# First block of a fused transformer kernel: input columns reordered, attention and gating worked between the chunks of the input projection, rotation read from PSUM on VectorE, retention last

## The chip, the cores and the metric

The kernel runs on one core of a Trainium2 chip. The metric is the device time of one execution in microseconds (us). TensorE is called PE, VectorE DVE, ScalarE ACT, GpSimd POOL, SyncE SP.

## The reference

A sequence of 256 tokens with 1024 channels passes through two layers of a first block (and then through a second block, which this change leaves as it is). Cut to what matters:

```python
def hybrid_layer(x, cos, sin, ...):
    h = rms_norm(x, g_mix_pre)
    z = h @ w_in                                   # 1024 -> 3200 columns
    rq, rk, rv, rg, aq, ak, av, gu, gv = split(z, [384]*7 + [256]*2)
    y_ret = silu(rg) * retention(rope(rq), rope(rk), rv)      # 6 heads of 64, group-normed
    y_att = dilated_attention(rope(aq), rope(ak), av)         # 6 heads of 64, causal softmax
    y_gm  = spatial_gating(gelu(gu), gelu(gv), w_s, b_s)      # u * (W_s norm(v) + b)
    y = concat([y_ret, y_att, y_gm])
    x = x + rms_norm(y @ w_out, g_mix_post)
    h = rms_norm(x, g_ffn_pre)
    gate, up = split(h @ w_gate_up)
    return x + rms_norm((silu(gate) * up) @ w_down, g_ffn_post)
```

A conditioning vector is also multiplied with `w_mod_2`, in three thirds for each layer ("mod0" to "mod2"), for use in the second block.

## The kernel before, in words

All arithmetic is float32. To run it on PE as three passes, each operand is cut into a high and a low part: high*high, high*low, low*high (lines 463 to 465 of `products`). Tokens are two tiles (t = 0, 1) of 128.

Weights stream in pieces called granules, two blocks of 128 rows by one chunk's columns. SP loads them in the order of a list, `ring`, into 8 raw slots (`load`, L418); a slot is loaded again only when the granule in it has been cut, or, for a mod granule (used uncut), multiplied. SP works through the list in order, so a slot that is not free holds up all later loads. ACT cuts the high part (`cut_high`, L426, or L429 with a gain), DVE the low part (`cut_low`, L436 or L439), into 4 slots: granule n can be cut only when PE is done with granule n-4.

A layer runs in this order. The input projection has 8 chunks of 400 columns in the order of `w_in`, 4 granules each; ACT copies each finished chunk from PSUM to `z`, scaled by the root of the norm (`take_z`, L2531). POOL rotates the retention columns and later the attention columns from `z` (`rope_tile`, L814 to L821). Retention is worked between chunks 3 to 7: transposes (L849), scores (L998, L999), decay on DVE (L1019), values (L925 to L927). After the last chunk `mix_pe`, `mix_act` and `mix_dve` do the rest: 24 transposes of the attention heads (L866), their cutting, then for each head scores (L1050, L1052), mask and maximum on DVE (L1207 to L1210), exponential on ACT (L1114, L1116), division on DVE (L1201), transposes (L1060), a copy by ACT (L1122), values (L1069 to L1071). The gating (gelu, norm, `wsT` product L1086) and mod0 (rows L953, columns L963) stand between the heads. Then y is transposed (L915), cut (L1129, L1234), and the output projection runs: 8 granules of 512 columns, the last four in two passes, one for each token tile, in `boundary_pe`. There mod1 rows (L953) stand between the last output and the first chunk of the feed-forward weights. Each engine's instructions run in the order written; DVE and ACT keep three granules ahead (`Cuts.to`).

PSUM has 8 banks. The chunks alternate between banks (0, 1) and (2, 3), named `MM`; the rest serve transposes, scores and outputs.

Of the kernel before, what the change touches and what calls it, by code (L numbers as in the profile page):

```python
# [7 lines left out]
F32 = mybir.dt.float32  # L8
# [163 lines left out]
def program(nc, a, out, tables):  # L172
    where = Where()
    ctx = ExitStack()
    with ctx:
# [22 lines left out]
        turned, turned_pool = xn[:, 0, 0:2 * RW], xn[:, 1, 0:2 * RW]  # L198
        logits = turned.rearrange("p (b s) -> p b s", b=2)
# [4 lines left out]
        a_q, a_k_high = hT_high, hT_low  # L204
# [19 lines left out]
        with mixer:  # L224
            z = sb("z", [P, NT, ZW], of=mixer)
            y = sb("y", [P, NT, D], of=mixer)
            qk = sb("qk", [P, NT, 4 * RW], of=mixer)
            qkT = sb("qkT", [P, NH, SEQ], of=mixer)
            a_k_low = sb("a_k_low", [P, NH, SEQ], F32R, of=mixer)
            seen = sb("seen", [P, NH, 384], of=mixer)  # L230
            gel = sb("gel", [P, NT, 2 * GMW], of=mixer)
            gel2 = sb("gel2", [P, NT, 2 * GMW], of=mixer)
            silu = sb("silu", [P, NT, RW], of=mixer)
            probT = sb("probT", [P, 2, 384], of=mixer)
        with ffn:
# [103 lines left out]
        IN_W, IN_CHUNKS, GU_CHUNKS = 400, 8, FK // 2  # L339
# [22 lines left out]
        MOD_LAST = (4, 5, 7, 8)  # L362
        OUT_ORDER = [(j, PAIRS[h]) for hs in ((0, 1), (2, 3)) for j in range(2) for h in hs]
# [4 lines left out]
        for layer in range(DEPTH):  # L368
            add_in(layer, range(1, IN_CHUNKS))
            add_mod(layer, 0)  # L370
            for j, rows in OUT_ORDER:
                w_out[layer].add(a["w_out"][layer], rows, 512 * j, 512).half = j
            add_mod(layer, 1, (0,))
# [258 lines left out]
        def x_root_pool(e, side, t, layer):  # L632
# [25 lines left out]
        def x_high_act(e, side, t, banks, layer):  # L658

            for j in range(2):  # L660
                e.wait_ge(pe.sem, pe.value(f"{side}_T{t}{j}", layer=layer))
                src, to = turned_half(t, j, banks)
                e.activation(hT_high[to], src, ACT.Copy).then_inc(act.sem, act.mark(f"{side}_H{t}{j}", layer))

        def x_low_dve(e, side, t, banks, layer):

            for j in range(2):
                e.wait_ge(act.sem, act.value(f"{side}_H{t}{j}", layer=layer))
                src, to = turned_half(t, j, banks)
                e.tensor_tensor(hT_low[to], src, hT_high[to].bitcast(F32),  # L670
                                ALU.subtract).then_inc(dve.sem, dve.mark(f"{side}_L{t}{j}", layer))
# [152 lines left out]
        def rope_tile(e, mine, t, z0, to, name, tmp, places=None):  # L824

            if t:
                e.wait_ge(mine.sem, mine.value(f"{name}{t - 1}"))
            src = heads(z[:, t, z0:z0 + 2 * RW], 2 * NH)
            dst = src if places else heads(to, 2 * NH)
            rope(e, mine, src, dst, 2 * NH, HD, cosf[:, t, :], sinf[:, t, :], tmp, f"{name}{t}", places)  # L830
# [6 lines left out]
        RT = (4, 5, 6)  # L837
        AT = (7, 6, 0, 1, 2, 3)

        def pairs_turn_pe(e, name, mine, first, banks, free):  # L840

            for t in range(NT):
                e.wait_ge(mine.sem, mine.value(f"{name}{t}"))
            for j in range(3):
                free(j)
                for pp in range(2):
                    for t in range(NT):
                        c = (first + 2 * j + pp) * P
                        last = e.transpose(PS[:, banks[j], pp * SEQ + t * P:pp * SEQ + (t + 1) * P],  # L849
                                           qk[:, t, c:c + P], ident)  # L850
                last.then_inc(pe.sem, pe.mark(f"{name}_T{j}"))

        def pairs_take_act(e, name, first, banks):
            for j in range(3):
                e.wait_ge(pe.sem, pe.value(f"{name}_T{j}"))
                c = first + 2 * j
                e.activation(qkT[:, c:c + 2, :], PS[:, banks[j], :].rearrange("p (a s) -> p a s", a=2),
                                      ACT.Copy).then_inc(act.sem, act.mark(f"{name}_qkT{j}"))

        def pairs_of_heads_pe(e):  # L860

            for i in range(NH):
                for half in range(2):
                    for t in range(NT):
                        h = 2 * i + half
                        last = e.transpose(PS[:, AT[i], half * SEQ + t * P:half * SEQ + (t + 1) * P],  # L866
                                           qk[:, t, h * P:(h + 1) * P], ident)
                last.then_inc(pe.sem, pe.mark(f"a_heads{i}"))

        def a_place(i):  # L870
            return slice(2 * (i % 3), 2 * (i % 3) + 2), PS[:, AT[i], :].rearrange("p (k s) -> p k s", k=2)

        def heads_high_act(e):
            e.wait_ge(granules_done, w_in[where.layer].last.cut + 1)
            for i in range(NH):
                e.wait_ge(pe.sem, pe.value(f"a_heads{i}"))
                ks, src = a_place(i)
                if i < 3:
                    last = e.activation(a_q[:, ks, :], src, ACT.Copy, scale=HD ** -0.5)
                else:  # L880
                    last = e.activation(a_k_high[:, ks, :], src, ACT.Copy)
                last.then_inc(act.sem, act.mark(f"a_high{i}"))

        def heads_low_dve(e):
            for i in range(NH):
                e.wait_ge(act.sem, act.value(f"a_high{i}"))
                ks, src = a_place(i)
                if i < 3:
                    rows = a_q[HD:P, ks, :]
                    last = e.scalar_tensor_tensor(rows, src[HD:P], HD ** -0.5, rows.bitcast(F32), ALU.mult, ALU.subtract)  # L890
                else:
                    last = e.tensor_tensor(a_k_low[:, ks, :], src, a_k_high[:, ks, :].bitcast(F32), ALU.subtract)
                last.then_inc(dve.sem, dve.mark(f"a_low{i}"))

        YB, OB, GB = (4, 5), (6, 7), 4

        Y_PLACES = ((0, 0), (0, SEQ), (1, 0), (OB[0], 0), (OB[0], SEQ), (OB[1], 0), (2, 0), (2, SEQ))


        Y_UNITS = (((0, 1), "y_T0"), ((2,), "y_T1"), ((3, 4), "y_T1"), ((5,), "y_T1"), ((6, 7), "y_T3"))  # L900

        def y_ready(e):
            def before(k, stream):
                if any(k == ks[0] for ks, _ in Y_UNITS):
# [2087 lines left out]
```

## Time and profile before

| | us |
|---|---|
| Three runs: lowest, median, highest | 1142.06, 1147.05, 1149.88 |
| Time of the profiled execution | 1141.9 |
| Its span, from the first to the last instruction | 1140.1 |
| PE busy (share of the span) | 1082.1 (95%) |
| DVE busy | 709.5 (62%) |
| ACT busy | 576.3 (51%) |
| POOL busy | 131.6 (12%) |

The profile is of one execution. Around its span lie 1.8 us. A busy PE is one with a product in its pipe; the ends of its instructions are modelled, so 95% says little of how fast products follow each other. That is read from their starts.

### The profile page before, as it was taken

The numbers are of one execution on the slowest core, as the hardware profiler recorded it, in microseconds if no ns is written. First come the engines' busy times: TensorE is split into PE (matmuls) and PEld (weight loads), VectorE is DVE, ScalarE is ACT, GpSimd is POOL, SyncE is SP. The second block draws the span as 40 slices with busy tenths as digits, with TensorE's granted clock in tenths as the row PEclk, the third lists the DMA queues.
The fourth block names the chain that finished last, engine by engine and source line by source line (L and its number), as shares of the span: only waits on it lengthen the run. The fifth ranks groups of instructions, "written<-read, shape, count | busy, mean of one in ns | idle before, by whom it ended". The sixth has DMA issues, their size and how long they took to land.

```text
span 1140.1 us, 15629 instructions
## 1 busy us (share of the span) xinstructions
PE 1082.1 (95%) x5974; PEld 893.2 (78%) x5974; DVE 709.5 (62%) x1162; ACT 576.3 (51%) x1054; POOL 131.6 (12%) x126
## 2 busy tenths in 40 slices
PE   7997899999999998799999999999998999999997
PEld 6896678888887997577888778889796678789785
DVE  5868756666545758766666536623256653876664
ACT  6644556555435554455555544434235643524772
POOL 1424010000001406001000000001000002022040
PEclk9999999999999999899999999999999999999999
DMA  8753568666665663459756494323211011344000
GB/s 299 238 146 95 188 202 274 185 184 182 186 182 196 227 174 109 154 177 351 234 178 184 138 343 138 86 84 116 74 57 55 1 57 56 129 124 136 1 2 37
DMA packets 109571, 170.45 MB, mean 150 GB/s; under 512 B 7213, under 2 KB 72762, under 8 KB 109242
## 3 DMA queue, kind: packets, MB, share of 16 engines
q1 hardware_dynamic: 107424, 161.92, 45.0%
q0 software_dynamic: 1440, 6.10, 1.5%
q10 hardware_dynamic: 634, 1.44, 0.3%
q8 instruction: 47, 0.77, 0.3%
q14 instruction: 26, 0.21, 0.1%
HBM read 168.39 MB, written 1.05 MB: 149 GB/s over the span
## 4 chain that ended last, share of the span: by engine, by line
PE 81%; DVE 12%; ACT 3%; issue 2%; DMA 1%; SPq 1%; DVEq 0%; POOLq 0%; POOL 0%; ACTq 0%
PE PS L463 16%; PE PS L465 16%; PE PS L464 16%; DVE low L439 5%; PE PS L2900 4%; PE PS L2901 4%; PE PS L2902 4%; PE PS L953 2%; PE PS L1699 1%; PE PS L1806 1%; PE PS L1382 1%; PE PS L1687 1%; PE PS L1644 1%; DVE low L436 1%; DMA ws_rows<-w_s 1%
## 5 line engine op out<-in xcount | busy, mean ns | idle before, releaser
L463 PE MATMUL PS<-high,hT_high 128*128 128x512 f32 (+3 forms) x860 | 329.9, 384 | 14.2 <-DVE low L439 7.8
L464 PE MATMUL PS<-low,hT_high 128*128 128x512 f32 (+3 forms) x860 | 324.2, 377 | 0.0
L465 PE MATMUL PS<-high,hT_low 128*128 128x512 f32 (+3 forms) x860 | 323.9, 377 | 0.0
L439 DVE SCALAR_TENSOR_TENSOR low<-raw,vec_cols,high 128x512 fp32r<-128x512 f32 (+1 forms) x304 | 232.9, 813 | 93.9 <-ACT high L429 93.8
L429 ACT ACTIVATE high<-raw,vec_cols 128x512 fp32r<-128x512 f32 (+1 forms) x304 | 190.1, 675 | 104.8 <-PE PS L465 102.3
L436 DVE TENSOR_TENSOR low<-raw,high 128x1024 fp32r<-128x1024 f32 (+2 forms) x118 | 139.0, 1186 | 162.9 <-ACT high L426 162.3
L426 ACT ACTIVATE high<-raw 128x1024 fp32r<-128x1024 f32 (+2 forms) x122 | 124.4, 1028 | 171.7 <-PE PS L465 92.3
L463 PEld LDWEIGHTS PS<-high,hT_high 128*128 128x128 f32 x860 | 162.0, 188 | 48.4 <-DVE low L439 14.1
L465 PEld LDWEIGHTS PS<-high,hT_low 128*128 128x128 f32 x860 | 161.9, 188 | 25.6
L464 PEld LDWEIGHTS PS<-low,hT_high 128*128 128x128 f32 x860 | 162.1, 188 | 23.6
L2900 PE MATMUL PS<-high,fT_high 128*128 128x512 f32 x176 | 70.4, 400 | 0.0
L2901 PE MATMUL PS<-low,fT_high 128*128 128x512 f32 x176 | 69.5, 395 | 0.0
L2902 PE MATMUL PS<-high,fT_low 128*128 128x512 f32 x176 | 69.5, 395 | 0.0
L463 PE MATMUL PS<-high,cT_high 128*128 128x512 f32 (+2 forms) x124 | 46.1, 372 | 0.0
L464 PE MATMUL PS<-low,cT_high 128*128 128x512 f32 (+2 forms) x124 | 45.9, 370 | 0.0
L465 PE MATMUL PS<-high,cT_low 128*128 128x512 f32 (+2 forms) x124 | 45.8, 369 | 0.0
L2900 PEld LDWEIGHTS PS<-high,fT_high 128*128 128x128 f32 x176 | 33.0, 188 | 11.0 <-issue 2.5
L621 POOL TENSOR_TENSOR norms<-norms,half_power 128x1 f32<-128x1 f32 x8 | 4.4, 552 | 318.8 <-DVE norms L613 318.8
L2902 PEld LDWEIGHTS PS<-high,fT_low 128*128 128x128 f32 x176 | 33.0, 187 | 8.1
L2901 PEld LDWEIGHTS PS<-low,fT_high 128*128 128x128 f32 x176 | 33.0, 188 | 7.6
L2253 DVE CUSTOM_DVE_ANT_0 z_late<-PS,consts,stats 128x512 f32<-128x512 f32 x32 | 22.8, 748 | 18.4 <-PE PS L1817 18.4
L2567 ACT ACTIVATE fT_high<-PS 128x512 fp32r<-128x512 f32 x22 | 13.2, 599 | 41.5 <-PE PS L2884 41.5
(359 smaller groups left out, 1560.7 us busy)
## 6 DMA issues: line engine op xcount, KB each, us to landing
raw<-w_gate_up SPq DMA_DIRECT2D x176, 256.0 KB
raw<-w_in SPq DMA_DIRECT2D x64, 400.0 KB
raw<-w_mod SPq DMA_DIRECT2D x48, 512.0 KB
raw<-w_down SPq DMA_DIRECT2D x44, 512.0 KB
raw<-o_w_in SPq DMA_DIRECT2D x20, 512.0 KB
raw<-w_out SPq DMA_DIRECT2D x16, 512.0 KB
raw<-e_w_in SPq DMA_DIRECT2D x12, 512.0 KB
raw<-e_w_out SPq DMA_DIRECT2D x8, 512.0 KB
```

Source lines behind the costliest of these rows:

```text
L426: last = e.activation(g.high, g.raw, ACT.Copy)
L429: last = e.activation(g.high[:, i, :], g.raw[:, i, :], ACT.Copy, scale=g.gain[:, i:i + 1])
L436: last = e.tensor_tensor(g.low, g.raw, g.high.bitcast(F32), ALU.subtract)
L439: last = e.scalar_tensor_tensor(g.low[:, i, :], g.raw[:, i, :], g.gain[:, i:i + 1], g.high[:, i, :].bitcast(F32), ALU.mult, ALU.subtract)
L463: e.matmul(bank, xh[:, k, tokens], g.high[:, i, :], start=first and i == 0, stop=False)
L464: e.matmul(bank, xh[:, k, tokens], g.low[:, i, :], start=False, stop=False)
L465: done = e.matmul(bank, xl[:, k, tokens], g.high[:, i, :], start=False, stop=last and i == len(g.rows) - 1)
L953: last = e.matmul(PS[at:at + 32, mod_place(third)[0][c], :], silu_c[:, k, :], g.raw[:, i, :], start=k < 4, stop=k >= 4)
L2253: e.tensor_tensor_reduce(o_logits[i % 4], PS[:, i % 2, :], late_const("window", NT)[:, t, :], -1.0, neg_sink[:, h:h + 1], ALU.add, ALU.min ...
L2900: e.matmul(bank, fT_high[:, n, tokens], g.high[:, 0, cols], start=n == 0, stop=False)
L2901: e.matmul(bank, fT_high[:, n, tokens], g.low[:, 0, cols], start=False, stop=False)
L2902: last = e.matmul(bank, fT_low[:, n, tokens], g.high[:, 0, cols], start=False, stop=n == FK - 1)
```

## The change

- **Order of columns.** `w_in` is taken as one chunk of 512 columns (the gating's gu and gv) and seven of 384: aq, ak, av, rq, rk, rv, rg. The pre-norm gain is applied to the transposed x (eight small operations for each token tile on ACT and on DVE), not to the weights, so that a granule is cut by one instruction on ACT and one on DVE.
- **Work between chunks.** A step s stands behind each of the 32 granules on PE, ACT and DVE (`mix_step_pe`, `mix_step_act`, `mix_step_dve`). Steps 4 to 18 hold the gating, steps 8 to 16 the rotation, transposes and cutting of the attention's q and k, steps 17 to 26 the six heads, steps 20 to 29 the rotation, transposes and scores of the retention.
- **mod0** granules stand ahead of `w_in` granules 7, 8, 10 and 11 in the ring, two each; PE multiplies them in steps 6, 7, 9 and 10.
- **Rotation** is by DVE, straight from PSUM, with the norm's root as a scalar: three instructions of PSUM data and one or two additions for each of aq, ak, rq, rk and each token tile. ACT doesn't copy these chunks, POOL does none of the rotation.
- **Mask and maximum** of a head are two `tensor_tensor_reduce` in place of one addition and two reductions.
- **Tail.** After the last chunk come the retention's values, then the output projection's four granules of the attention and gating rows (4 to 7), then mod1 rows of the first half (taken out of the boundary), the transposes of the retention's y, and the four granules of rows 0 to 3, for which DVE centres, norms and gates y meanwhile.
- The PSUM banks of outputs and of x's transposes move with it.

```diff
--- before.py
+++ after.py
...
-        IN_W, IN_CHUNKS, GU_CHUNKS = 400, 8, FK // 2
+        IN_COLS = ((Z_GU, 2 * GMW), (Z_AQ, RW), (Z_AK, RW), (Z_AV, RW), (Z_RQ, RW), (Z_RK, RW), (Z_RV, RW), (Z_RG, RW))
+        IN_CHUNKS, GU_CHUNKS = len(IN_COLS), FK // 2
+        MOD_AHEAD = {7: (0, 0), 8: (0, 1), 10: (1, 0), 11: (1, 1)}
...
-                for rows in PAIRS:
-                    w_in[layer].add(a["w_in"][layer], rows, c * IN_W, IN_W, pre_gain(V_MIX, layer, rows))
+                for h, rows in enumerate(PAIRS):
+                    if 4 * c + h in MOD_AHEAD:
+                        of, half = MOD_AHEAD[4 * c + h]
+                        add_mod(layer, 0, (of,), PAIRS[2 * half:2 * half + 2])
+                    w_in[layer].add(a["w_in"][layer], rows, *IN_COLS[c])
...
+        MIX_ORDER = [(j, PAIRS[h]) for hs in ((2, 3), (1, 0)) for j in range(2) for h in hs]
...
+            for n, (j, rows) in enumerate(MIX_ORDER):
+                if n == 4:
+                    add_mod(layer, 1, (0,))
...
+                if side == "mix":
+                    last = e.activation(hT_high[to], src, ACT.Copy)
+                else:
+                    for i in range(4):
+                        k = 4 * j + i
+                        last = e.activation(hT_high[:, k, t * P:(t + 1) * P], src[:, i, :], ACT.Copy, scale=mix_gain(layer, k))
...
+            half = HD // 2
+            e.scalar_tensor_tensor(tv[:, :, 0:half], src[:, :, half:HD], r, table(sinf[:, t, 0:half]), ALU.mult, ALU.mult)
+            e.scalar_tensor_tensor(tv[:, :, half:HD], src[:, :, 0:half], r, table(sinf[:, t, half:HD]), ALU.mult,
+                                   ALU.mult).then_inc(dve.sem, dve.mark(f"{name}_sin{t}"))
+            e.scalar_tensor_tensor(dst, src, r, table(cosf[:, t, :]), ALU.mult, ALU.mult).then_inc(dve.sem, dve.mark(f"{name}_cos{t}"))
+            e.wait_ge(dve.sem, dve.value(f"{name}_cos{t}"))
+            if both:
+                for _, place in twice(to, NH):
+                    last = e.tensor_tensor(place, dst, tv, ALU.add)
+            else:
+                last = e.tensor_tensor(dst, dst, tv, ALU.add)
+            last.then_inc(dve.sem, dve.mark(f"{name}{t}"))
 
...
+        MOD_MIX = {6: (0, 0), 7: (0, 1), 9: (1, 0), 10: (1, 1)}
+
+        def mix_step_pe(e, s):
+
+            if s in MOD_MIX:
+                if s == 6 and where.layer == 0:
+                    e.wait_ge(dve.sem, dve.value("silu_c"))
+                    e.wait_ge(dve.sem, dve.value("wsT"))
+                c, half = MOD_MIX[s]
+                mod_rows_pe(e, 0, c, slice(2 * half, 2 * half + 2))
+            elif s == 11:
+                heads_turn_pe(e, "aq", lambda j: None)
+            elif s == 12:
+                e.wait_ge(act.sem, act.value("mod0_rows1"))
+                for c in range(2):
+                    mod_columns_pe(e, 0, c)
+            elif s == 14:
...
+            if 17 <= s < 17 + NH:
+                att_scores(e, s - 17)
+            if 19 <= s < 19 + NH:
+                att_turn(e, s - 19)
+            if 20 <= s < 20 + NH:
+                att_values(e, s - 20)
+            if s == 26:
+                for t in range(NT):
+                    e.wait_ge(dve.sem, dve.value(f"rk{t}"))
+                e.wait_ge(dve.sem, dve.value(f"logits{NH - 1}"))
+                e.wait_ge(act.sem, act.value(f"probT{NH - 1}"))
+                e.wait_ge(dve.sem, dve.value("ya_L1"))
...
+            elif s in (28, 29):
+                for h in range(3 * (s - 28), 3 * (s - 27)):
+                    ret_scores(e, h)
...
+        def att_scores(e, h):
+
+            if h == 0:
+                e.wait_ge(dve.sem, dve.value("ak_L2"))
+            if h >= 2:
+                e.wait_ge(dve.sem, dve.value(f"logits{h - 2}"))
+            bank = 4 + h % 2
+            for part, k in enumerate((a_k_high, a_k_low)):
+                e.matmul(PS[:, bank, 0:P], a_q[:, h, 0:P], k[:, h, 0:P], start=part == 0, stop=part == 1)
+            for part, k in enumerate((a_k_high, a_k_low)):
+                last = e.matmul(PS[:, bank, P:384], a_q[:, h, P:SEQ], k[:, h, :], start=part == 0, stop=part == 1)
+            last.then_inc(pe.sem, pe.mark(f"scores_a{h}"))
+
+        def att_turn(e, h):
+
+            e.wait_ge(dve.sem, dve.value(f"weights{h}"))
+            if h:
+                e.wait_ge(act.sem, act.value(f"probT{h - 1}"))
+            for b in range(3):
+                last = e.transpose(PS[:, 6, b * P:(b + 1) * P], a_prob(h)[:, b * P:(b + 1) * P], ident)
+            last.then_inc(pe.sem, pe.mark(f"turned{h}"))
+
+        def att_values(e, h):
+
+            e.wait_ge(act.sem, act.value(f"probT{h}"))
+            if h == 0:
+                e.wait_ge(dve.sem, dve.value("yg_L"))
+            elif h == 4:
+                e.wait_ge(dve.sem, dve.value("logits4"))
...
+        def ret_turn_pe(e):
+
+            for ks, name in (((2,), "y_T2"), ((0, 1), "y_T0")):
+                for t in range(NT):
+                    e.wait_ge(dve.sem, dve.value(f"ret_done{t}"))
+                for k in ks:
+                    bank, at = Y_RET[k]
+                    for t in range(NT):
+                        last = e.transpose(PS[:, bank, at + t * P:at + (t + 1) * P], y_ret[:, t, k * P:(k + 1) * P], ident)
+                last.then_inc(pe.sem, pe.mark(name))
...
+            if 18 <= s < 18 + NH:
+                h = s - 18
+                e.wait_ge(dve.sem, dve.value(f"logits{h}"))
+                if h >= 3:
+                    e.wait_ge(pe.sem, pe.value(f"turned{h - 3}"))
+                for t, cols in enumerate((slice(0, P), slice(P, 384))):
+                    last = e.activation(a_prob(h)[:, cols], logits[:, h % 2, cols], ACT.Exp, scale=-1.0,
+                                        bias=neg_max[:, h, t:t + 1], accum_out=denom[:, h, t:t + 1])
...
+            if 20 <= s < 20 + NH:
+                h = s - 20
+                e.wait_ge(pe.sem, pe.value(f"turned{h}"))
...
+            cuts.to(granules[5])
+            mod_rows_act(e, 1, 0)
+            e.wait_ge(pe.sem, pe.value("y_T2"))
+            e.activation(hT_high[:, 2, :], PS[:, Y_RET[2][0], 0:SEQ], ACT.Copy).then_inc(act.sem, act.mark("y_H2"))
+            e.wait_ge(pe.sem, pe.value("y_T0"))
+            e.activation(hT_high[:, 0:2, :], PS[:, Y_RET[0][0], :].rearrange("p (k s) -> p k s", k=2), ACT.Copy).then_inc(act.sem, act.mark("y_H0"))
...
+            elif s in (8, 9):
+                rope_step_dve(e, "aq", s - 8)
...
+                rope_step_dve(e, "ak", 0)
+            elif s == 13:
+                rope_step_dve(e, "ak", 1)
+                mod_take_dve(e, 0)
...
+                for t, cols in enumerate((slice(0, P), slice(P, 384))):
+                    last = e.tensor_tensor_reduce(logits[:, h % 2, cols], PS[:, 4 + h % 2, cols], const("log_seen")[:, cols], -1.0,
+                                                  3.0e38, ALU.add, ALU.min, neg_max[:, h, t:t + 1])
+                last.then_inc(dve.sem, dve.mark(f"logits{h}"))
...
+            if s in (20, 21):
+                rope_step_dve(e, "rq", s - 20)
+            elif s in (24, 25):
+                rope_step_dve(e, "rk", s - 24)
...
+        def mix_tail_dve(e, cuts, granules):
+
+            e.wait_ge(pe.sem, pe.value(f"values_r{NH - 1}"))
+            centred(e, "ret", ret_values(), ret_heads(y_ret), 12, HD)
...
             cuts.to(granules[3])
+            spread(e, "ret", ret_heads(y_ret), ret_heads(gel2[:, :, 0:RW]), 12, HD, 16, EPS)
+            cuts.to(granules[4])
+            e.wait_ge(pool.sem, pool.value("ret_var"))
+            rs = small[:, 16:28].rearrange("p (t g) -> p t g", t=NT).unsqueeze(3).broadcast_to([P, NT, NH, HD])
...
+                e.scalar_tensor_tensor(y_ret[:, t, :], y_ret[:, t, :], norm("ffn", t, S_HALF), silu[:, t, :],
+                                       ALU.mult, ALU.mult).then_inc(dve.sem, dve.mark(f"ret_done{t}"))
+            cuts.to(granules[5])
+            e.wait_ge(act.sem, act.value("y_H2"))
+            e.tensor_tensor(hT_low[:, 2, :], PS[:, Y_RET[2][0], 0:SEQ], hT_high[:, 2, :].bitcast(F32),
...
+            for s in range(4 * IN_CHUNKS):
+                cuts.to(w_in[layer].granules[s], 3)
...
+                mix_step_act(e, s)
+            mix_tail_act(e, cuts, w_out[layer].granules)
...
-            mod_rows_pe(e, third, 0)
+            if third != 1:
+                mod_rows_pe(e, third, 0)
...
+                if c == 2:
+                    e.wait_ge(act.sem, act.value(f"zg{t}"))
+                elif c == 5:
+                    e.wait_ge(act.sem, act.value(f"zav{t}"))
+                elif c > 2:
+                    e.wait_ge(dve.sem, dve.value({3: "aq", 4: "ak", 6: "rq", 7: "rk"}[c] + str(t)))
...
+                    mix_step_pe(e, 4 * c + h)
...
+            for h in range(NH):
+                values_pe(e, seen[:, h, :], h, r_v, YB, f"values_r{h}")
...
+                    done = out_products(e, g, t, PS[:, OUT_BANKS[t][g.half], :], g.rows[0] == 4, False)
...
+            mod_rows_pe(e, 1, 0)
+            ret_turn_pe(e)
...
-        OUT_BANKS = ((3, 4), (5, 2))
+        OUT_BANKS = ((0, 4), (1, 7))
...
```

## Rows read from the trace of the kernel before

**Rows 1.** The page, part 1: busy us of each engine, share of the span, instructions

```profile
PE 1082.1 (95%) x5974; PEld 893.2 (78%) x5974; DVE 709.5 (62%) x1162; ACT 576.3 (51%) x1054; POOL 131.6 (12%) x126
```

**Rows 2.** Busy us in three stretches: layer 0's mixing, its last part, a feed-forward stretch

```profile
core 0: us, PE busy (x) PEld busy (x) DVE busy (x) ACT busy (x) POOL busy (x), PEclk, DMA share, GB/s
19.00:136.00 117.00, 100.61 (x604) 90.47 (x602) 89.70 (x149) 64.30 (x134) 34.70 (x20) 0.97 0.53 171
100.00:136.00 36.00, 25.05 (x168) 17.55 (x168) 26.36 (x62) 19.40 (x52) 3.08 (x2) 0.91 0.35 121
200.00:236.00 36.00, 36.00 (x162) 29.12 (x161) 24.36 (x38) 20.27 (x34) 0.00 (x0) 1.00 0.61 185
```

**Rows 3.** Timeline of PE: start us, us, instruction; the ends of four stages

```profile
19.14 0.43 PE L463 MATMUL PS<-high,hT_high 128*128 128x400 f32 x1
136.09 0.47 PE L463 MATMUL PS<-high,hT_high 128*128 128x512 f32 x1 [1.99 <-DVE hT_low L1234]
358.51 0.45 PE L463 MATMUL PS<-high,hT_high 128*128 128x400 f32 x1
484.32 0.47 PE L463 MATMUL PS<-high,hT_high 128*128 128x512 f32 x1 [1.99 <-DVE hT_low L1234]
```

**Rows 4.** Timeline of PE: further products of the three widths

```profile
25.57 0.34 PE L465 MATMUL PS<-high,hT_low 128*128 128x400 f32 x1
...
488.83 0.40 PE L464 MATMUL PS<-low,hT_high 128*128 128x512 f32 x1
...
762.29 0.34 PE L463 MATMUL PS<-high,hT_high 128*128 128x384 f32 x1
764.20 0.34 PE L465 MATMUL PS<-high,hT_low 128*128 128x384 f32 x1
```

**Rows 5.** Timeline of PE: the pieces of the mixing

```profile
53.07 1.47 PE L849 MATMUL PS<-consts,qk 128*128 128x128 f32 x12
63.20 0.71 PE L998 MATMUL PS<-qkT 64*128 64x256 f32 x4
76.87 0.33 PE L925 MATMUL PS<-z,seen 128*128 128x64 f32 x2
80.61 0.39 PE L927 MATMUL PS<-z,seen 128*128 128x64 f32 x2
159.54 1.92 PE L953 MATMUL PS<-raw,silu_c 128*32 128x512 f32 x16
371.11 1.84 PE L963 MATMUL PS<-consts,mod_block 128*128 128x2 f32 x16
473.42 0.43 PE L1069 MATMUL PS<-probT,z 128*64 128x128 f32 x2
474.95 0.28 PE L1052 MATMUL PS<-a_k_low,hT_high 128*128 128x256 f32 x1
```

**Rows 6.** Timeline of DVE and POOL: low cuts with and without POOL's rotation

```profile
38.12 2.07 POOL L821 TENSOR_TENSOR qk<-qk,xn 128x768 f32<-128x768 f32 x1
38.39 6.98 DVE L439 SCALAR_TENSOR_TENSOR low<-raw,vec_cols,high 128x400 fp32r<-128x400 f32 x4
71.77 1.18 DVE L439 SCALAR_TENSOR_TENSOR low<-raw,vec_cols,high 128x400 fp32r<-128x400 f32 x2 [2.83 <-ACT high L429]
```

**Rows 7.** Groups by line and form, DVE: busy us, mean ns, idle before

```profile
L1207 DVE TENSOR_TENSOR xn<-PS,consts 128x384 f32<-128x384 f32 x12 | 6.7, 555 | 9.8 <-PE PS L1052 9.8
L436 DVE TENSOR_TENSOR low<-raw,high 128x768 fp32r<-128x768 f32 x6 | 5.7, 957 | 25.1 <-ACT high L426 25.1
```

**Rows 8.** Timeline of POOL: the root for the retention's norm, layer 1

```profile
446.74 2.94 POOL L695 TENSOR_TENSOR small<-small,half_power 128x12 f32<-128x12 f32 x1 [3.67 <-DVE small L1164]
```

**Rows 9.** Timeline around mod1's rows in layer 0's boundary: DVE and PE

```profile
163.56 1.41 DVE L629 SCALAR_TENSOR_TENSOR x_now<-o_gained,norms,x_now 128x512 f32<-128x512 f32 x2
166.49 0.48 PE L463 MATMUL PS<-high,hT_high 128*128 128x512 f32 x1
```

**Rows 10.** DMA issues to 140 us: count, KB each, median us to landing

```profile
ws_rows<-w_s SPq DMA_DIRECT2D x1, 512.0 KB, 10.0
```

**Rows 11.** SP's waits in the first 200 us: us in total, times, longest

```profile
SPq L418 <- PE PS L953: 34.6, 7, 14.0
```

More of the change, by code:

```diff
@@ L842, in pairs_turn_pe, with heads_turn_pe @@
+        A_BANKS, R_BANKS, R_SCORES = (4, 5, 6), (5, 6, 7), (4, 7, 5, 6, 4, 7)
+        YB, GB = (5, 6), 7
+        Y_ATT = ((7, 0), (7, SEQ), (4, 0))
+        Y_RET = ((2, 0), (2, SEQ), (3, 0))
+        def heads_turn_pe(e, name, free):
             for t in range(NT):
-                e.wait_ge(mine.sem, mine.value(f"{name}{t}"))
+                e.wait_ge(dve.sem, dve.value(f"{name}{t}"))
             for j in range(3):
                 free(j)
[L846 to L862, printed above, removed]
@@ L873, in heads_high_act @@
[L873 to L893, printed above, removed]
@@ new lines, in out_products @@
+        def out_products(e, g, t, bank, first, last):
+            tokens = slice(t * P, (t + 1) * P)
+            for i, k in enumerate(g.rows):
+                xh, xl = y_operand(k)
+                e.matmul(bank, xh[:, tokens], g.high[:, i, :], start=first and i == 0, stop=False)
+                e.matmul(bank, xh[:, tokens], g.low[:, i, :], start=False, stop=False)
+                done = e.matmul(bank, xl[:, tokens], g.high[:, i, :], start=False, stop=last and i == len(g.rows) - 1)
+            return done
@@ new lines, in att_turn @@
+        def att_turn(e, h):
[11 more added lines that the diff above has]
+                e.wait_ge(dve.sem, dve.value("logits4"))
+            rows, (bank, at) = slice(h % 2 * HD, (h % 2 + 1) * HD), Y_ATT[h // 2]
+            to = PS[rows, bank, at:at + SEQ]
+            v = [a_v[:, t, h * HD:(h + 1) * HD] for t in range(NT)]
+            e.matmul(to[:, 0:P], v[0], probT[:, h % 2, 0:P], start=True, stop=True)
+            e.matmul(to[:, P:SEQ], v[0], probT[:, h % 2, P:2 * P], start=True, stop=False)
+            last = e.matmul(to[:, P:SEQ], v[1], probT[:, h % 2, 2 * P:3 * P], start=False, stop=True)
+            last.then_inc(pe.sem, pe.mark(f"values_a{h}"))
@@ new lines, in mix_tail_act @@
+        def mix_tail_act(e, cuts, granules):
+            for t in range(NT):
+                chunk_ready(e, w_in[where.layer], "in", IN_CHUNKS - 1, t)
+                e.wait_ge(pool.sem, pool.value(f"ffn_half{t}", layer=where.layer - 1))
+                e.activation(silu[:, t, :], PS[:, MM[1][t], 0:RW], ACT.Tanh,
+                             scale=norm("ffn", t, S_HALF)).then_inc(act.sem, act.mark(f"rg_tanh{t}"))
+            cuts.to(granules[5])
[4 more added lines that the diff above has]
+            e.activation(hT_high[:, 0:2, :], PS[:, Y_RET[0][0], :].rearrange("p (k s) -> p k s", k=2), ACT.Copy).then_inc(act.sem, act.mark("y_H0"))
@@ L1175, in mix_dve @@
             sq4 = gel2[:, :, 0:GMW].rearrange("p t (g d) -> p t g d", g=NG)
[L1177 to L1180 removed]
+            if s == 4 and where.layer:
+                where.layer -= 1
+                mod_take_dve(e, 2)
+                where.layer += 1
```

586 lines of the change are left out of this document (261 added, 325 removed).

## Prediction

> **What bounds the kernel now.** The page's busy shares come first: PE 95%, DVE 62%, ACT 51%, POOL 12% [rows 1]. PE is the bound over the whole, but the share is an average, so the windows come next. In a feed-forward stretch PE has no gap and clock 1.00; in layer 0's mixing it is busy 100.6 of 117 us, and in the last part, where attention is worked with no weights' products beside it, 25.1 of 36 us at a granted clock of 0.91: a mix of the 2.4 GHz level and, after its waits, the 1.2 GHz level. POOL's 34.7 us stand almost all in the same 117 us [rows 2]. The timeline of PE then gives the lengths that I compare: from the second tile of chunk 0 to the first output product 117.0 us in layer 0 (19.14 to 136.09), and from the first product of chunk 0 to the first output product 125.8 us in layer 1 (358.51 to 484.32) [rows 3]. Both output projections begin after 1.99 us of waiting for DVE. Thus some 35 us of each layer are a chain through PE, DVE and ACT in turn, not a sum of products, and the projection ahead of it has DVE near its limit where POOL works too.
>
> **Products of the projection.** Starts follow each other by 0.184 us at 400 columns ((25.57 - 19.14)/35), 0.237 us at 512 ((488.83 - 484.32)/19) and 0.174 us at 384 ((764.20 - 762.29)/11) [rows 3, 4]. Before: 384 x 0.184 = 70.5 us a layer. After: 48 x 0.237 + 336 x 0.174 = 11.4 + 58.3 = 69.7 us. The widths are worth nothing: -0.8.
>
> The Trainium skill, page "TensorE: Matmul & The Clock Gate", section "Back-to-back issue gap", gives N/2.4 + 2.5 ns for an isolated gap. By it 384 columns would take 162.5 ns, 400 169.2 and 512 215.8, so 65.0 us before and after; the rows here are 11 to 21 ns slower, and go into the sum. By either the regrouping is no gain.
>
> **The mixing on PE, now between granules.** Spans at full clock, pipe included [rows 5]: three sets of 12 transposes (aq, ak, retention) at 1.47 and four for the gate, 4.9 us; mod0 rows 2 x 1.92 = 3.8; its columns 1.8; the `wsT` product, eight instructions at the transposes' rate, 1.0; a head's values, transposes and scores 1.8 (473.42 to 475.23), six of them 10.9; retention scores 0.8 for two heads, 2.4; its values 4.1 (76.87 to 81.00), now after the last chunk. Sum 28.9. That much PE can't avoid; only the waits around it go.
>
> **Waits that stay.** A granule of 384 columns takes PE 12 x 0.174 = 2.1 us. ACT may cut granule s+3 only when PE is done with s-1, DVE follows, and then comes DVE's work of step s, so that it is ready at best 2 us after PE's granule s-1, about when granule s ends. I walked steps 6 to 31 with the durations of the rows. (a) Steps 8, 9, 12 and 13 give DVE a rotation each beside gelu, norm and low cuts, some 4 us where PE takes 2.1 to 4; three granules of lead cover it, but PE's gate product in step 14 waits for `gate_norm`, queued behind both ak rotations: 1 us, with the chunk's remaining products queued behind it. (b) In steps 19 to 23 `att_turn` waits for `weights` and for the last `probT`; what DVE and ACT have queued (cut, mask, exponential, division, and in steps 20 and 21 the rotation of rq) takes 0.3 to 1 us longer than PE's step of 3.9: 3 us in all. (c) The first mod rows wait for `silu_c` in layer 0, and loads held up by mod granules delay cuts of granules 10 and 11, 1 us. Together 5 us a layer. Bounds: 1 (every wait covered) and 14 (see the rivals).
>
> **DVE's load.** Low cuts: 28 at 0.96, four of 1024 elements at 4/3 of that, 32 us a layer [rows 7]. A rotation is new: 384 elements from PSUM take 0.56 [rows 7]; the two sine halves read 192 each, between 0.28 and 0.56, taken as 0.35; one or two additions at 0.55: 1.8 to 2.4 a tile, eight tiles 17 us, bounds 14 to 24. The rest is about what it was, some 24 us (of 26.4 in the last part [rows 2] less output cuts, with the decay). `tensor_tensor_reduce` is in no row; between a plain addition (0.56 for both tiles) and addition plus two reductions of like size, 1.7; I take 0.8, nearer the addition. In all some 73 us in a stage of 105, against 89.7 in 117 before [rows 2]. DVE has room as a sum. What pays for the rotation is POOL: low cuts took 6.98/4 = 1.75 us each while POOL rotated (38.12) and 0.59 without [rows 6], and that stretching goes.
>
> **Start.** ws_rows lands 10.0 us after its issue, behind eight loads [rows 10], and PE needs it before the second tile of chunk 0. The eight loads now hold a tenth more bytes of all that must land by then; I take 1.6 us later, between 0 and 3. The eight small gain operations in place of two are hidden in the boundary behind mod2 rows, and partly in that 1.6 at the start.
>
> **The sum, layer 0.** Second tile of chunk 0 begins at 19.1 + 1.6 = 20.7; its products 5.7; chunks 1 to 7 58.3; mixing 28.9; waits 5: output products at 118.6, against 136.1: -17.5. **Layer 1:** chunk 0 11.4, x's transposes, mod2 rows and columns beside it 4.7, chunks 58.3, mixing 28.9, waits 5: 108.3 against 125.8: -17.5.
>
> **Tail and boundary.** After its values the retention's chain on DVE is about 2.1 centring, 1.1 gating, 1.2 + 1.2 for two cuts of 1024 elements, 2.1 squares and sums, POOL's root 2.94 [rows 8] partly beside a cut (1.7 left), 2 for the norm and gate: 11.5 us. PE has four output granules, 48 x 0.237 = 11.4, and mod1 rows 1.9, 13.3 us: covered by 1.8, and without the mod rows not. Then come six transposes 0.7 and the cut of y's third block on ACT and DVE, behind mod1's copy on ACT: 0.8 of waiting. The mod rows leave the boundary, but there the first feed-forward chunk waits for DVE in any case (its fourth granule starts at 166.49, after the residual of 163.56 to 164.97 has been transposed [rows 9]): 0.2 back. So +1.9 + 0.7 + 0.8 - 0.2 = +3.2 a layer, bounds 1 and 6.
>
> Sum: 2 x (-17.5 + 3.2) = -28.6. On the profiled execution, 1141.9 with 1.8 around its span, that is 1113.3; the median of the three runs stands 5.2 higher, so 1118.5; forecast 1118.
>
> **Rivals.** *The chain comes along* (0.22): DVE and ACT, each in program order, pass every head's chain on late, so that PE loses 2 us at each of six heads and 3 at the rotations, 15 a layer in place of 5: 1138 at its end, 1128 halfway. For it: DVE had 26.4 busy of the last 36 us; against it: 73 of 105 as a sum. *Everything is covered* (0.06): waits 1, tail 1: 1147.05 - 2 x 20.5 = 1106 or less. *It does not do what it says* (0.07): PE's waits of the last part come back in full between the granules (11 us a layer of idle [rows 2], plus 3 at a lower clock), 1137 to 1150. *Slower* (0.05), by the ring: a mod granule holds its raw slot until PE's step, and SP, in order, can't load what lies behind; SP already waited 34.6 us for L953, 14.0 at once [rows 11]. If at each of the four mod steps the next `w_in` granule lands after PE's lead is used up, PE stands still for a whole landing, up to the 10.0 us of rows 10; the gain of 14.3 a layer is gone at 3.6 us a step, and at 6 it gives 1147.05 + 19 = 1166. Against it: granules 10 and 11 have three granules of lead, 6 us and more.
>
> **Chances and range.** Forecast case 0.60, with 1106 to 1128 as its own range. A measurement tells about 1% of 1147 from no change, 1135.6 to 1158.5. Faster by over 1%: 0.60 + 0.06 + 0.20 of the first rival + 0.02 = 0.88; within 1% 0.07; slower 0.05. The range of 8 in 10, 1104 to 1136, takes in the bounds of the waits (-4 to +9 a layer, not both at an end) and most of the first rival.
>
> **What would show it.** PE's first output product in layer 0 near 118.6 and the layer 1 stage near 108 long; granted clock near 1.00 in both; no POOL rotation and no low cut over 1.3 us; the gap ahead of `wsT`'s product near 1 us, those ahead of the heads' transposes below 1; a rotation of 1.8 to 2.4 a tile; first product of y's row blocks 2 and 3 about 0.8 after the last transpose. It is wrong if `tensor_tensor_reduce` or the sine halves, with their strided PSUM reads, take twice what I assume, if `w_in` cuts wait for DMA, or if the retention's chain outlasts 13.3 us.

## The result, and the profile after

The changed kernel takes 1138.14 us in the median (1135.78 to 1140.20, seven runs) against 1144.21 (1141.84 to 1149.88, seven runs): ratio 0.9939, 95% interval 0.9918 to 0.9959. It is faster, by 6 us (under 1%), where 29 were forecast. The profiled execution took 1137.99, with a span of 1136.2 against 1140.1 before.

The page of the changed kernel, parts 1 and 2 (to be held against [rows 1]):

```profile
PE 1085.5 (96%) x5974; PEld 890.5 (78%) x5974; DVE 688.2 (61%) x1206; ACT 551.1 (49%) x990; POOL 77.3 (7%) x94
...
PEclk9889999999999999999999999999999999999999
```

DVE, ACT and POOL have lost the work that they were to lose, and the time hardly moved. So I read the two stages next, with the cuts at the events that the prediction used (second tile of chunk 0 to the first output product; in layer 1 from the first product of chunk 0). The table of windows of the changed kernel; columns are length, busy time of PE, of its weight loads (PEld), of DVE, ACT and POOL, granted clock, DMA share, GB/s:

```profile
20.84:133.46 112.62, 100.75 (x597) 89.66 (x596) 71.94 (x156) 51.83 (x93) 2.92 (x3) 0.94 0.55 186
359.42:476.26 116.84, 108.94 (x663) 95.27 (x659) 75.54 (x155) 55.29 (x102) 8.07 (x10) 0.97 0.62 207
```

DVE's 72 us are the 73 of the forecast, down from 89.7 [rows 2]. But PE is still idle for 11.9 us in layer 0 (112.62 - 100.75) and 7.9 in layer 1, and at the granted clock of 0.94 and 0.97 it loses another 0.06 x 100.75 = 6.0 and 0.03 x 108.94 = 3.3 (an estimate from these rows). Idle and clock together are 17.9 and 11.2 us where the forecast had waits of 5. A table of windows by ten microseconds shows where:

```profile
30.00:40.00 10.00, 6.26 (x30) 4.28 (x30) 5.75 (x11) 4.66 (x7) 0.00 (x0) 0.79 0.36 129
40.00:50.00 10.00, 8.17 (x45) 6.57 (x48) 1.52 (x2) 3.12 (x4) 0.00 (x0) 0.87 0.87 308
50.00:60.00 10.00, 9.55 (x62) 7.33 (x63) 9.86 (x18) 5.45 (x8) 0.00 (x0) 1.00 0.80 263
60.00:70.00 10.00, 6.58 (x44) 6.25 (x42) 9.80 (x21) 2.53 (x3) 2.32 (x1) 1.00 0.53 162
70.00:80.00 10.00, 9.22 (x44) 9.16 (x45) 5.86 (x12) 3.24 (x6) 0.00 (x0) 0.66 0.32 95
```

The heads and the retention behind them lose little: from 80 to 134 PE is busy 52.4 of 54 us at a clock of 1.00 (row not shown). The loss lies in steps 6 to 15. Between 30 and 40 DMA is at a share of 0.36: the weights are not late because the transfers are at their limit (the next ten microseconds reach 0.87); they haven't been asked for. The timelines of SP and of ACT in that stretch say why (start, duration, and in brackets the idle time before and what ended it):

```profile
24.45 3.02 SPq L433 DMA_DIRECT2D raw<-w_in  x2
28.90 10.13 SPq L433 DMA_DIRECT2D raw<-w_mod  x2
39.07 0.47 SPq L433 DMA_DIRECT2D raw<-w_in  x1
39.59 4.58 SPq L433 DMA_DIRECT2D raw<-w_mod  x2
```

```profile
34.49 0.84 ACT L441 ACTIVATE high<-raw 128x768 fp32r<-128x768 f32 x1 [0.64 <-DMA raw<-w_in]
43.39 0.84 ACT L441 ACTIVATE high<-raw 128x768 fp32r<-128x768 f32 x1 [8.06 <-DMA raw<-w_in]
44.14 1.04 ACT L1146 ACTIVATE gel<-gel 128x1024 f32<-128x1024 f32 x1
48.57 0.84 ACT L441 ACTIVATE high<-raw 128x768 fp32r<-128x768 f32 x1 [3.38 <-DMA raw<-w_in]
```

SP stands for 10 us between two loads of `w_mod`: the raw slots of the first mod granules come free only when PE has multiplied them in step 6, at 36.68, after a wait of 3.74 for `silu_c`, the conditioning vector that the mod rows are multiplied with. `w_in` granule 10 stands behind and is issued at 39.07; ACT cuts it at 43.39, after standing idle for 8.06 us. Everything that ACT and DVE have queued behind that cut is late with it. PE's waits in the two stages (line, what it waited for, us in total, times, longest), layer 0 first:

```profile
PE PS L1033 <- DVE gel L1269: 4.2, 1, 4.2
PE PS L978 <- DVE silu_c L2778: 3.7, 1, 3.7
PE PS L978 <- ACT mod_row L994: 1.8, 1, 1.8
PE PS L1088 <- ACT probT L1178: 1.0, 1, 1.0
```

```profile
PE PS L1033 <- DVE gel L1269: 3.2, 1, 3.2
PE PS L978 <- ACT mod_row L994: 2.8, 1, 2.8
```

L1033 is `wsT`'s product in step 14, L1269 `gate_norm` (DVE's last operation on the gate's values ahead of that product), L994 ACT's copy of the mod rows. No line of PE in these stages names DMA: the transfer is two engines away, and only ACT's waits (for `w_in`, ahead of its cuts: 14.8 us in layer 0, 12.6 in layer 1) show it.

### The profile page after: what moved, and what is told of

Same layout as the page of the kernel before. It is cut to its first block, busy times and chain, and to the rows that moved or that the text cites. A ratio compares the mean times of both kernels' runs of the same rounds, so it can differ in the third digit from the quotient of the medians.

```text
span 1136.2 us, 15595 instructions
## 1 busy us (share of the span) xinstructions
PE 1085.5 (96%) x5974; PEld 890.5 (78%) x5974; DVE 688.2 (61%) x1206; ACT 551.1 (49%) x990; POOL 77.3 (7%) x94
## 4 chain that ended last, share of the span: by engine, by line
PE 81%; DVE 10%; ACT 4%; issue 3%; DMA 2%; SPq 0%; DVEq 0%; POOLq 0%; POOL 0%; ACTq 0%
PE PS L478 15%; PE PS L479 15%; PE PS L480 15%; PE PS L2974 4%; PE PS L2975 4%; PE PS L2976 4%; DVE low L451 2%; PE PS L978 2%; DMA raw<-w_in 1%; PE PS L1811 1%; ACT high L441 1%; PE PS L940 1%; PE PS L941 1%; PE PS L942 1%; PE PS L1918 1%
## 5 line engine op out<-in xcount | busy, mean ns | idle before, releaser
L451 DVE TENSOR_TENSOR low<-raw,high 128x1024 fp32r<-128x1024 f32 (+3 forms) x182 | 202.0, 1116 | 224.1 <-ACT high L441 223.5
L478 PE MATMUL PS<-high,hT_high 128*128 128x512 f32 (+2 forms) x796 | 309.6, 389 | 7.8 <-DVE low L451 5.5
L441 ACT ACTIVATE high<-raw 128x1024 fp32r<-128x1024 f32 (+3 forms) x186 | 180.2, 975 | 271.4 <-PE PS L480 148.7
L479 PE MATMUL PS<-low,hT_high 128*128 128x512 f32 (+2 forms) x796 | 301.5, 379 | 0.0
L480 PE MATMUL PS<-high,hT_low 128*128 128x512 f32 (+2 forms) x796 | 301.3, 378 | 0.0
L478 PEld LDWEIGHTS PS<-high,hT_high 128*128 128x128 f32 x796 | 151.8, 191 | 49.1 <-issue 11.4
L480 PEld LDWEIGHTS PS<-high,hT_low 128*128 128x128 f32 x796 | 151.9, 191 | 24.2
L454 DVE SCALAR_TENSOR_TENSOR low<-raw,vec_cols,high 128x512 fp32r<-128x512 f32 x176 | 124.2, 747 | 51.7 <-ACT high L444 51.7
L444 ACT ACTIVATE high<-raw,vec_cols 128x512 fp32r<-128x512 f32 x176 | 117.0, 714 | 46.6 <-PE PS L480 44.7
L978 PE MATMUL PS<-raw,silu_c 128*32 128x512 f32 x192 | 25.8, 634 | 8.3 <-ACT mod_row L994 4.6
```

The lines of the kernel that those rows point to most:

```text
L441: last = e.activation(g.high, g.raw, ACT.Copy)
L444: last = e.activation(g.high[:, i, :], g.raw[:, i, :], ACT.Copy, scale=g.gain[:, i:i + 1])
L451: last = e.tensor_tensor(g.low, g.raw, g.high.bitcast(F32), ALU.subtract)
L454: last = e.scalar_tensor_tensor(g.low[:, i, :], g.raw[:, i, :], g.gain[:, i:i + 1], g.high[:, i, :].bitcast(F32), ALU.mult, ALU.subtract)
L478: e.matmul(bank, xh[:, k, tokens], g.high[:, i, :], start=first and i == 0, stop=False)
L479: e.matmul(bank, xh[:, k, tokens], g.low[:, i, :], start=False, stop=False)
```

## The experiments

Theory A is the reading above: a mod granule holds its raw slot until PE's step, and the loads behind it come late. Theory B: DVE's own queue of rotations, gating and cuts is the limit. Theory C: the bandwidth of the weights' transfers is. All times below are medians of four runs, each against the kernel before on the same chip.

**Order of loads alone.** In the changed kernel `MOD_AHEAD` gives the `w_in` granules ahead of which mod0 stands in the ring; PE's steps for it stay.

```diff
-        MOD_AHEAD = {7: (0, 0), 8: (0, 1), 10: (1, 0), 11: (1, 1)}
+        MOD_AHEAD = {10: (0, 0), 11: (0, 1), 13: (1, 0), 14: (1, 1)}
```

> Only the order of loads changes: mod0's granules stand ahead of w_in granules 10, 11, 13 and 14 instead of 7, 8, 10 and 11; what PE, ACT and DVE do, and in which order, is the same. Theory A (the slots: a mod granule keeps its raw slot until PE's step, SP waits for it in order, so w_in granules 10 to 16 are loaded too late, and everything that DVE has behind their cuts comes late): the waits of ACT for w_in (14.8 us in layer 0, 12.6 in layer 1) fall below 4, PE's wait for the gate product (4.2 and 3.2) falls to 1 or less, the granted clock of the stage stays near 1.00, layer 0's stage falls from 112.4 to about 102 (a wait for silu_c stays), layer 1's from 117.0 to about 109: 1119 to 1124. Theory B (DVE's own queue of rotations, gating and cuts is the limit, and the late loads only cover it): the waits for w_in go, PE's gate wait stays at 3 or more, 1131 to 1136. Theory C (HBM's bandwidth is the limit in this stage): the same bytes, no change, 1137 to 1139.

The same edit by one (8, 9, 11, 12) and by five (12, 13, 15, 16):

> Only the order of loads, as in the first kernel but by one granule: mod0 ahead of w_in 8, 9, 11 and 12. Theory A with its count of slots: w_in granule 11 can now be loaded only after PE's step 6 and is wanted for cutting when step 7 is done, one step after; in the changed kernel granule 10 came free at step 6 and was wanted at step 6. So about half the loss is left: ACT's waits for w_in 5 to 9 us a layer, PE's gate wait 1.5 to 3, 1125 to 1132, between the changed kernel (1138) and the move by three (1119). If the cause were another (one particular granule, or a step between none and some late loads), it would lie at one of the ends.

> The same move by five granules (ahead of w_in 12, 13, 15 and 16). Theory A: as with three, within 1 us, if mod0 lands in time for PE's steps 6 and 7; if it doesn't, PE now waits for w_mod itself, 2 to 6 us a layer, 1124 to 1132. Theories B and C as before.

| mod0 later by | median us | ratio, 95% interval | ACT waits for `w_in`, layers 0, 1 | PE ahead of `wsT`'s product | PE for `w_mod` |
|---|---|---|---|---|---|
| 0 (the change) | 1138.14 | 0.9939 (0.9918 to 0.9959) | 14.8, 12.6 | 4.2, 3.2 | 0 |
| 1 | 1128.62 | 0.9852 (0.9823 to 0.9881) | 8.6, 8.1 | 3.2, 3.5 | 0 |
| 3 | 1119.36 | 0.9762 (0.9731 to 0.9792) | 0, 0 | 0.9, 1.0 | 0 |
| 5 | 1128.11 | 0.9828 (0.9797 to 0.9860) | 0, 0 | 0.8, 0.8 | 2.0, 2.6 |

Windows of the kernel with three, cut at the same events:

```profile
22.22:124.29 102.07, 96.51 (x597) 86.64 (x596) 71.75 (x156) 51.83 (x93) 2.31 (x1) 0.98 0.61 201
350.23:458.89 108.66, 105.73 (x662) 92.78 (x659) 75.44 (x155) 55.66 (x102) 8.06 (x10) 1.00 0.66 223
```

With not one instruction changed on PE, ACT, DVE or POOL, the stages are 10.6 and 8.2 us shorter (Theory A: 10 and 8), DVE has the same 71.8 us of work, and the wait for `gate_norm`, though nothing of DVE's order was touched, falls to 1. Of the 10.6 us in layer 0, 6.3 are idle time of PE and 4.2 busy time, as the granted clock rises from 0.94 to 0.98. Theory C is excluded (same bytes, 19 us less) and B as the main cause (it had 1131 or more). The granule count behind A holds as well: by one, half the loss is left. There PE's wait for mod rows is gone, but its wait for `gate_norm` stays at 3.2 and 3.5, above the 1.5 to 3 expected. By five the other side comes: mod0 itself lands late. PE's waits for it (2.0 and 2.6) are about half of the 4.2 and 4.7 us by which the stages are longer than with three; its busy time is up by 2.3 and 2.2, in layer 0 nearly all of it in the mod rows (6.8 us in place of 4.3).

**Order in DVE's queue.**

```diff
@@ mix_step_dve, s == 12: after the low cuts of aq
+                e.wait_ge(pool.sem, pool.value("gate_var"))
+                rs = ...
+                e.tensor_tensor(vg, vg, rs, ALU.mult)...mark("gate_norm")
                 rope_step_dve(e, "ak", 0)
             elif s == 13:
+                mod_take_dve(e, 0)
                 rope_step_dve(e, "ak", 1)
-                mod_take_dve(e, 0)
-                e.wait_ge(pool.sem, pool.value("gate_var"))
-                ...
```

> Loads as in the changed kernel. DVE's gate_norm stands ahead of the first rotation of ak (step 12) instead of behind the second (step 13), modT0 ahead of the second rotation. Theory A (late loads hold up DVE as a whole): PE's gate product waits 2.2 to 4.4 us less (one or two rotations), so this wait goes, but the later ones of the ak transposes take part of it back: 1131 to 1135. Theory B (order within DVE's queue is the cause): the 4.2 and 3.2 us and the 3 us of low clock behind the first go: 1127 to 1130.

> Both edits: mod0 three granules later in the ring, and gate_norm ahead of the rotations. Theory A: within 1.5 us of the first kernel (the reordering is worth nothing once the loads come in time). Theory B: 4 us or more below it.

Measured 1131.93 (ratio 0.9867, 0.9835 to 0.9898) with the loads of the change, and 1116.67 (0.9742, 0.9714 to 0.9769) with mod0 three later. The first is A's 1131 to 1135; PE still waits there for `modT0` (2.0 and 1.0) and for the mod rows (2.0 and 2.6). The second is 2.7 below the one with the loads alone, between A's 1.5 and B's 4, with intervals that overlap: what the order adds is close to the 1.9 us of waiting that was left. With the loads late the same order was worth 6.2 us by the medians (8 by the ratios): it takes back a third of what the late loads cost, without touching them, and most of that is no longer there to be had once they come in time.

**silu_c.** DVE makes it in step 5, not 6 (`EARLY = {1: 1, 2: 2, 4: 3, 5: 4}`), on top of both edits; then the same with mod0 four later; then alone in the changed kernel:

> On top of the kernel with both edits: DVE makes silu_c (its fourth early step) in step 5 and not in step 6, where it was queued behind the cut of granule 9. In the kernel with both edits PE waited 2.97 us for silu_c and ran its next products of layer 0 at a pitch of the 1.2 GHz level up to about 41. Theory A (the waits add up on PE's path and each brings a stretch of low clock): the wait falls to 1, and most of the low clock goes: 2 to 4 us, 1113 to 1115. Rival: the next wait takes its place (granules 7 to 9, or landing of w_mod), 0 to 1 us, 1116 to 1117.

> As the one before, with mod0 ahead of w_in granules 11, 12, 14 and 15 (four later than in the changed kernel). Theory A: w_in never waits (2.9 us of ACT at one granule of layer 1 before, off PE's path), but w_mod lands just when PE wants it: with five it was late by 2.0 and 2.6 us. Between 0 and +4 against the one before: 1113 to 1118.

> The changed kernel with only silu_c made in step 5 instead of step 6. There PE waited 3.7 us for it in step 6, and SP held back w_in granule 10 until that step. Theory A (a wait ahead of a mod step is paid twice, by PE and by the loads behind the slot): earlier release of the slots as well, layer 0 gains 3 to 6 us, layer 1 nothing: 1132 to 1135. Rival (the landing of granule 10 sets the pace in any case, the wait only covers it): 1136 to 1139.

Measured 1113.81 (ratio 0.9725, 0.9698 to 0.9752), 1115.11 (0.9734, 0.9701 to 0.9767), and alone 1132.42 (0.9871, 0.9851 to 0.9890). Alone it gives 5.7 us by the medians (7.8 by the ratios), more than the 3 us that PE waits less for it (3.7 to 0.8). Theory A had the size, 3 to 6, and the rival (1136 to 1139) is out; but the reason that A gave, that the loads behind the slot pay the wait a second time, is not borne out. The stage of layer 0 and PE's waits in it:

```profile
21.28:128.21 106.93, 97.44 (x597) 87.44 (x596) 71.85 (x156) 51.70 (x93) 2.75 (x2) 0.97 0.59 194
PE PS L1033 <- DVE gel L1269: 4.2, 1, 4.2
PE PS L978 <- ACT mod_row L994: 2.4, 1, 2.4
...
PE PS L978 <- DVE silu_c L2778: 0.8, 1, 0.8
```

The two waits that the late loads cause are no shorter than in the change (4.2 and 2.4, against 4.2 and 1.8), though ACT's wait for `w_in` falls from 14.8 to 10.0. Of the 5.7 us 2.4 are idle time of PE and 3.3 its busy time, at a granted clock of 0.97 in place of 0.94: the second payment is the low clock that followed the wait of 3.74. Four granules are 1.3 us longer than three by the medians, with overlapping intervals. 1113.81 is the fastest kernel here, 24 us below the change; its stages:

```profile
22.14:119.35 97.21, 94.75 (x597) 85.37 (x596) 71.69 (x156) 51.61 (x93) 2.32 (x1) 1.00 0.64 210
345.29:452.67 107.38, 105.47 (x663) 92.81 (x659) 75.56 (x155) 55.68 (x102) 8.07 (x10) 1.00 0.68 226
```

**POOL.** Is it true that taking the rotation off POOL pays for it on DVE? In the fastest kernel POOL gets idle work:

```diff
             inverse_root_pool(e, "gate_var", small[:, 28:36])
+            e.memset(pool_work[:, :], 1.0)...mark("work0")
+            for n in range(14):
+                e.wait_ge(pool.sem, pool.value(f"work{n}"))
+                e.tensor_tensor(pool_work[:, :], pool_work[:, :], pool_work[:, :], ALU.mult)...
```

> On top of the kernel with mod0 three later, gate_norm first and silu_c early (1113.8 us): POOL multiplies a tile of 128 x 768, which nothing else uses, 14 times with itself, after the gate's root (step 11), in each layer; in the kernel before, POOL's additions of that size took 2.07 us each, so some 29 us a layer, beside the later rotations, the heads and their cuts. It tests the prediction's claim that taking the rotation off POOL pays for its place on DVE. If the claim holds: DVE's low cuts beside it take 1.2 to 1.8 us instead of 0.955, DVE's busy time in the stage rises from 73 by 8 to 16 us, and PE's waits by 3 to 8 a layer: 1120 to 1130. Rival: DVE has slack enough in steps 11 to 22, the cuts stretch but PE doesn't wait: 1114 to 1116. Second rival: nothing stretches, and the slow cuts of the kernel before had another cause.

Measured 1130.25 (0.9850, 0.9832 to 0.9868): 16.4 us more by the medians, 14 by the ratios, just at the upper end of the 1120 to 1130 expected, for some 26 us of POOL in each layer that nobody waits for. The two stages are 8.4 and 7.8 us longer, and DVE is busy 81.3 us in layer 0's in place of 71.7. DVE by groups (line, tiles, shape, count, busy us, mean ns, idle before), 55 to 88, first with POOL busy, then without:

```profile
L452 DVE TENSOR_TENSOR low<-raw,high 128x768 fp32r<-128x768 f32 x9 | 15.1, 1698 | 2.5 <-ACT high L442 2.5
L872 DVE TENSOR_TENSOR qk<-rope_part 128x384 f32<-128x384 f32 x4 | 4.6, 1191 | 0.1
L1287 DVE TENSOR_TENSOR a_k_low<-PS,a_k_high 128x512 fp32r<-128x512 f32 x3 | 1.9, 673 | 0.0
L1298 DVE CUSTOM_DVE_ANT_0 xn<-PS,consts 128x256 f32<-128x256 f32 x3 | 1.2, 413 | 0.0
L865 DVE SCALAR_TENSOR_TENSOR rope_part<-PS,norms,sinf 128x192 f32<-128x192 f32 x3 | 1.2, 410 | 0.0
```

```profile
L451 DVE TENSOR_TENSOR low<-raw,high 128x768 fp32r<-128x768 f32 x11 | 10.4, 954 | 5.5 <-ACT high L441 5.5
L1293 DVE CUSTOM_DVE_ANT_0 xn<-PS,consts 128x256 f32<-128x256 f32 x5 | 2.1, 419 | 0.0
L871 DVE TENSOR_TENSOR qk<-rope_part 128x384 f32<-128x384 f32 x4 | 2.1, 555 | 0.1
L1282 DVE TENSOR_TENSOR a_k_low<-PS,a_k_high 128x512 fp32r<-128x512 f32 x3 | 1.9, 682 | 0.0
L864 DVE SCALAR_TENSOR_TENSOR rope_part<-PS,norms,sinf 128x192 f32<-128x192 f32 x4 | 1.6, 411 | 0.0
```

The cuts go from 954 to 1698 ns and the additions from 555 to 1191; both read two SBUF tiles. What reads one operand from PSUM, the rotation's products among it, keeps its time within 2%. PE then waits 3.5 us ahead of a head's transposes and runs at a clock of 0.90 in that stretch. The prediction's claim that POOL's work stretches DVE's holds; a kernel that leaves the rotation itself on POOL was not run. The Trainium skill, page "SBUF — State Buffer", section "Who interferes with whom", says that DVE with two SBUF inputs contends with a GpSimd instruction that reads SBUF and that with at most one, outside its 2-port perf modes, it doesn't; these rows agree on both counts.

## Why the prediction was wrong

| stage, us | before | forecast | the change | mod0 +3 | fastest |
|---|---|---|---|---|---|
| second tile of chunk 0 begins | 19.14 | 20.7 | 20.84 | 22.22 | 22.14 |
| layer 0, from there to first output product | 116.95 | 97.9 | 112.62 | 102.07 | 97.21 |
| first output product to first transpose of x | 21.08 | | 24.73 | 24.73 | 24.73 |
| layer 1, first product to first output product | 125.81 | 108.3 | 116.84 | 108.66 | 107.38 |

- **The step that failed** is *Waits that stay*, (c): "loads held up by mod granules delay cuts of granules 10 and 11, 1 us", and behind it the sentence that dismissed the ring: "granules 10 and 11 have three granules of lead, 6 us and more". Those three granules are the lead of cutting over multiplying. What matters is the lead of loading over cutting (the time from the issue of a load to the moment at which ACT may cut it), and for `w_in` granule 10 it is below zero: counted along the ring, the second mod granule has position 8 and granule 10 has position 16, the same raw slot; the slot comes free in PE's step 6, and ACT may cut granule 10 when PE is done with granule 6, just before. A landing lies between: 4.3 us from the issue at 39.07 to the cut at 43.39, and up to 5.3 for granule 11 in layer 1, issued at 387.30 and cut at 392.58. In place of the 1 us, ACT waited 14.8 and 12.6 us for `w_in`, and moving these loads alone made the two stages 10.6 and 8.2 us shorter. Counting slots would have shown it without a chip. The mechanism stood among the rivals (*slower, by the ring*, 0.05), with the right price of a few us a step; what was wrong was its weight and its end. The two stages gained 13.3 us in place of the 36.6 forecast, and the order of the loads accounts for 18.7 of the 23.3 that are missing. It deserved to widen the bounds of the main case.
- **Waits, the size**: 5 a layer forecast, 17.9 and 11.2 measured with the loads as they are. With mod0 three later layer 0 has 5.6 us of idle time and 1.9 of clock, layer 1 2.9 and none; in the fastest kernel 2.5 and 1.9. (a) `gate_norm`: 1 us forecast, 4.2 and 3.2 measured, 0.9 and 1.0 once the loads come: right, with the cause removed. (b) heads: 3 forecast, 1.5 measured. (c) `silu_c` 3.0 to 3.8 where I had put it into 1, together with the loads. The sum had no term for the granted clock, which cost 6.0 and 3.3 us.
- **Start**: +1.6 forecast, +1.7 measured in the change; it is 3.0 to 3.1 in the two other kernels of the table, whose PE ran at the lower clock level until 17.6 or later, the change's until 15.6. The run with `silu_c` alone, with the change's loads, begins at 21.28: part of the difference is spread between executions.
- **Mixing and products on PE**: too low by some 2 us a layer. Without its 5 us of waits the forecast is 92.9 and 103.3; in the fastest kernel, at a clock of 1.00, PE is busy 94.75 and 105.47. That the stages of 97.21 and 107.38 lie so near 97.9 and 108.3 is luck: the waits there are 2.5 and 1.9, below the 5. Which piece was priced too low is open. These 2 us a layer are 4 of the 23.3 that are missing; the other 19 are waits and clock.
- **DVE's load**: 73 forecast, 71.9 measured in layer 0. Eight rotations take 17.7 us (forecast 17); a head's mask and maximum 0.70 (forecast 0.8).
- **Tail and boundary**: +3.2 forecast; 24.73 - 21.08 = +3.65, less 0.16 in the boundary (from the turn of x's first tile to the first product behind the turn of its second, 9.16 against 9.32 [rows 9]), +3.5 a layer. The retention's chain is covered but for 0.76 us ahead of y's last rows, as forecast (0.8).
- **Rivals**: the time of 1138 lies where "the chain comes along" and "does not do what it says" meet, but by neither mechanism: DVE and ACT don't pass each head's chain on late, and the last part's waits are gone. The measured time lies 2 us above the range (1104 to 1136), and a time within 1% of no change had been given 0.07.
- **What would show it**: "if `w_in` cuts wait for DMA" was the sign named, and it is the one that came.

The change against the kernel before, stage by stage: start +1.7, layer 0 -4.3, tail +3.5, layer 1 -9.0, tail +3.5: -4.6 by the last feed-forward layer (its last products begin at 707.0 against 711.5), -3.9 in the span. Where the last 0.6 is lost I did not follow.

## What to carry to other kernels

In a ring that is loaded in order, put a slot that is held long so far back that the load which inherits it is issued a landing ahead of its cut: count positions, not granules of lead, and look at the DMA share beside the wait: here it was 0.36 while the weights were late, because nobody had asked for them, and 0.87 once they were asked for. An operation moved into a dense stage brings its loads with it, and their place in the queue is a choice of its own (three granules were worth 19 us, five lost 9 of them again). The long wait on the engine that bounds the kernel was paid twice here, once as idle time and once in the clock that fell after it (`silu_c` alone: 2.4 us and 3.3).

## What the runs showed of the hardware

- After its long waits PE ran at the lower clock level for a while: in layer 0 of the change that added 6.0 us to 11.9 of idle time. PE's timeline of the changed kernel after the 4.20 us at the gate's product; starts 0.96 us apart for three products are 0.32 each, the 1.2 GHz level, where 384 columns otherwise take 0.174:

```profile
70.78 2.04 PE L1033 MATMUL PS<-gel,wsT 128*128 128x128 f32 x8 [4.20 <-DVE gel L1269]
...
73.58 0.52 PE L478 MATMUL PS<-high,hT_high 128*128 128x384 f32 x1
...
74.54 0.52 PE L478 MATMUL PS<-high,hT_high 128*128 128x384 f32 x1
...
75.50 0.52 PE L478 MATMUL PS<-high,hT_high 128*128 128x384 f32 x1
```

 After a wait of 0.81 us (for `silu_c` in the fastest kernel) and after one of 1.83 (for the mod rows in the change) products followed each other by 0.174: it did not fall. The length of a wait alone does not decide it: with `gate_norm` first it fell after 1.99 us (granted clock 0.57 from 69 to 73), with `silu_c` alone it did not after 2.39.
- POOL's products on one SBUF tile stretch DVE's instructions with two SBUF inputs by 1.8 to 2.1 times, and leave those with one PSUM operand as they are, within 2%: reading PSUM directly saves the copy, and it avoids the contention as well.
- Mask, addition and maximum in one `tensor_tensor_reduce` cost 0.28 us at 128 columns and 0.42 at 256.
